# The rolling transfers of the caches, issued inside the forming of a chunk's weights

## The reference, cut to what matters

```
def conv_ffn(h, conv_state, w_up, w_conv, b_conv, w_down):
    u = h @ w_up
    gate, up = u[..., :D_FF], u[..., D_FF:]
    ext = concatenate([conv_state, gate], axis=1)
    conv = ext[:, 0:S] * w_conv[0] + b_conv + ...
    act = silu(conv) * up
    return act @ w_down, ext[:, S:]
...
k_all = concatenate([k_buf, ka], axis=1)
new_k = k_all[:, k_all.shape[1] - keep:]
```

## Time and profile before

| what | value |
|---|---|
| median of three runs | 3106.83 us |
| the profiled execution: its time, and the span of its trace | 3108.89 us, 3107.3 us |
| PE busy | 2867.4 us, 92% of the span |
| DVE, ACT, POOL busy | 1874.3, 1042.3, 675.9 us |
| matmuls of the chunks (L1116), of w_down (L1192) | 673.3 + 252.1 us, 517.8 us |
| POOL idle ahead of L877, the first instruction of form, until weights land | 367.4 us, 32 times |
| rolls: issues, size, median from issue to landing | 8 + 8, 4088 KB, 15.1 and 14.9 us |
| mean granted clock of TensorE, share of full speed | 0.965 |

### The profile page before, as it was taken

How to read it: one execution, slowest core, us unless ns; L and a number is a source line. 1 busy time by engine, 2 the same in 40 slices (tenths; PEclk the granted TensorE clock), 3 DMA queues, 4 the chain that set the end, 5 groups by cost and what they waited for, 6 DMA issues and landing times. The chain is left out here.

```text
span 3107.3 us, 52590 instructions
## 1 busy us (share of the span) xinstructions
PE 2867.4 (92%) x20746; PEld 2630.0 (85%) x20746; DVE 1874.3 (60%) x3293; ACT 1042.3 (34%) x1833; POOL 675.9 (22%) x472
## 2 busy tenths in 40 slices
PE   8999999899898898999989999888998898899998
PEld 7888899689898898999987666555998898899998
DVE  3445344545977777755643444585378778786565
ACT  4444212333322222355533333222242222224544
POOL 3111222003432323101121000141144333330000
PEclk9999999999999999999999999998999999999999
DMA  6211111851244353577712000275213344435776
GB/s 192 60 58 56 36 42 49 324 182 55 80 146 163 122 170 119 176 215 224 216 60 82 15 1 9 99 305 224 68 42 116 129 162 149 135 123 181 221 223 210
DMA packets 280689, 406.87 MB, mean 131 GB/s; under 512 B 21914, under 2 KB 218548, under 8 KB 272884
## 3 DMA queue, kind: packets, MB, share of 16 engines
q1 hardware_dynamic: 272056, 295.32, 29.9%
q0 software_dynamic: 8448, 108.93, 9.8%
HBM read 357.66 MB, written 112.19 MB: 151 GB/s over the span
## 5 line engine op out<-in xcount | busy, mean ns | idle before, releaser
L1116 PE MATMUL psum<-mlp_halves,mlp_operands 128*128 128x352 f32 x3840 | 673.3, 334 | 99.7 <-DVE mlp_combine L1495 89.1
L1116 PEld LDWEIGHTS psum<-mlp_halves,mlp_operands 128*128 128x128 f32 x3840 | 651.8, 198 | 105.5 <-DVE mlp_combine L1495 93.7
L1192 PE MATMUL psum<-mlp_ring 128*128 128x352 f32 x3168 | 517.8, 324 | 6.4 <-issue 3.6
L1192 PEld LDWEIGHTS psum<-mlp_ring 128*128 128x128 f32 x3168 | 511.0, 188 | 8.9 <-issue 6.5
L920 DVE TENSOR_TENSOR mlp_ring<-mlp_ring_whole,mlp_ring 128x864 fp32r<-128x864 f32 x264 | 286.2, 1091 | 205.4 <-ACT mlp_ring L914 204.3
L1905 PE MATMUL psum<-h_ab,w_in_halves 128*128 128x352 f32 x2016 | 341.3, 326 | 3.3 <-PEq L281 2.3
L1905 PEld LDWEIGHTS psum<-h_ab,w_in_halves 128*128 128x128 f32 x2016 | 322.6, 189 | 17.1 <-issue 10.9
L914 ACT CAST mlp_ring<-mlp_ring_whole 128x864 fp32r<-128x864 f32 x264 | 241.1, 915 | 272.8 <-DMA mlp_ring_whole<-products_spill 272.5
L1116 PE MATMUL psum<-mlp_turns,mlp_operands 128*128 128x352 f32 x1440 | 252.1, 324 | 10.1 <-DVE mlp_operands L867 10.1
L1116 PEld LDWEIGHTS psum<-mlp_turns,mlp_operands 128*128 128x128 f32 x1440 | 235.3, 190 | 10.9 <-DVE mlp_operands L867 10.9
L607 PE MATMUL psum<-mlp_halves,project_w 128*128 128x352 f32 x1152 | 189.6, 327 | 8.3 <-DVE project_w L635 8.3
(11 more groups left out here) (372 smaller groups left out, 4311.3 us busy)
## 6 DMA issues: line engine op xcount, KB each, us to landing
mlp_ring_whole<-in_w_down SPq DMA_DIRECT2D x264, 256.0 KB, 2.8
mlp_ring_whole<-products_spill SPq DMA_DIRECT2D x264, 176.0 KB, 3.6
mlp_raw<-in_w_up SPq DMA_DIRECT2D x66, 512.0 KB, 7.0
out_new_a_k_s<-in_cache_a_k POOLq DMA_DIRECT2D x8, 4088.0 KB, 15.1
out_new_a_v_s<-in_cache_a_v POOLq DMA_DIRECT2D x8, 4088.0 KB, 14.9
products_spill<-window SPq DMA_DIRECT2D x44, 528.0 KB, 4.1
w_in_raw<-in_w_in_ab SPq DMA_DIRECT2D x28, 512.0 KB, 4.6
mlp_raw_up<-in_w_up SPq DMA_DIRECT2D x22, 512.0 KB, 3.8
```

Of the source, the lines that this page charges most:

```text
L1116: mm = nc.tensor.matmul(c.bank[bank][:, 0:TILE], operands[:, operand, w, k, :], tokens(x, k), start=begin and k + w + x == 0, stop=end and ...
L1192: mm = nc.tensor.matmul(c.bank[bank_set(at) + o][:, 0:TILE], slot[:, w, o * P:(o + 1) * P], slot[:, x, self.WIDE:], start=k + w + x == 0, ...
```

## The change

The roll is no longer the first thing of the pass. Function form takes a further argument, begun, and calls it after the first of its five instructions; in the pass's first refill, the forming of (g, 1), it issues the roll there, after both waits for the chunk's weights. The wait for the roll moves to the pass's second refill, the forming of (g+1, 0), again ahead of its last sum.

```
-    def form(self, pool, g, s, waits):
+    def form(self, pool, g, s, waits, begun=None):
...
         self.wait_gate(pool, g, s)
         self.wait_up(pool, g, s)
         waits(self.SUM_2)
         tt(into(self.SUM_2), whole(self.UP_1), whole(self.UP_2), ALU.add).then_inc(self.formed, 1)
+        if begun:
+            begun()
         pool.wait_ge(self.formed, done + 1)
...
-                def refill(g, s, next_g, next_s, rolled=None):
+                def refill(g, s, next_g, next_s, begun=None, rolled=None):
...
-                    self.form(pool, next_g, next_s, waits)
+                    self.form(pool, next_g, next_s, waits, begun)
...
                 with pool.Fori(0, DEC_BATCH) as i:
-                    roll.roll(pool, i, call)
-                    refill(i + 2, 0, i + 2, 1, lambda: roll.wait_rolled(pool, i, call))
-                    refill(i + 2, 1, i + 3, 0)
+                    refill(i + 2, 0, i + 2, 1, lambda: roll.roll(pool, i, call))
+                    refill(i + 2, 1, i + 3, 0, None, lambda: roll.wait_rolled(pool, i, call))
```

## The result

The changed kernel takes 2976.97 us in the median of four runs (2973.74 to 2979.97). The kernel before takes 3104.86 us, now over four runs, one more than above (3102.39 to 3109.22): a ratio of 0.9586, interval 0.957 to 0.9603. The prediction was 2978 us, faster.

A forecast was written before the change was run, and what follows sets the result against it. The prediction took the bound to be a gate load waiting out the roll, both released by one event, with PE stalling later. 3106.8 - 129.0 = 2978 us, the added issue and moved wait costed at nothing; range 2968 to 3040 us.

The forecast's parts named there:

- the most to be won: Loops over the groups: sixteen passes take 800.7 us, 671.7 without a stall, so at most 129.0 us to win.
- The gate load's landing: Next gate load, (3, 0), beside the first roll: lands 0.9 to 4.2 us behind the roll's 873.4, taken as 877.
- POOL's spare 0.5 us: POOL asks for the next gate load at 877.5, after P6 of (2, 1), 0.5 us after its forecast landing.
- the 2.3 us to spare: ACT asks for the next gate load at 879.3, for GATE_1, 2.3 us after its forecast landing.
- DVE's room: DVE's seventh sum in an unstalled chunk ends 5.4 us before P2 on PE needs it, a reserve for late loads.
- L + 4.3 - 5.4: PE's wait per pass, gate load L us late for ACT; 4.3 from POOL's sums falling together, 5.4 DVE's room.
- the clock's price: After a PE stall, the next 24 matmuls run at the lower clock, some 1.9 us more per pass.
- The second rival: Part of the stall remains: gate load 3.0 us late for ACT, 3.8 us a pass, 3039 us; chance 0.11.
- The stall that moves unchanged: The roll meets the next gate load, landing at 885.9, 6.6 us late for ACT: 3107 us; chance 0.03.
- the drain one by one: It gets slower: up load, store, gate load follow the roll singly, some 4 us each: 3163 us; chance 0.06.
- The late start of a roll's descriptors: Within the second rival: roll starts 3.4 us later, GpSimd being shut out of its port while writing descriptors.
- the moved wait: Ahead of the last sum of (g+1, 0), some 30 us after the issue, twice the roll's time: costs nothing.

## Why the prediction was right

**What bounds it, and the most to be won.** 129.0 us from the length of a pass against two chunks; the span fell by 128.9. Without the rolls the time is the changed kernel's, so the rolls were all that stood in the pass; with half of their bytes at the old place it is the same again, so it was the late gate load and not the collision as such.

**The gate load's landing.** Predicted 877 in the times before, which run some 0.6 us ahead of those after (835.15 against 835.78): 877.6 in the new ones, measured 877.35. Two terms of it were off and made up for each other. That is luck. The roll took 16.4 to 18.7 us, median 17.2, not 15.0; and the gate load was alone behind it, as the up load had landed at 861.1 and the store some 0.5 us ahead of the roll, so that it landed 1.5 us behind the roll where the forecast had 3.6. With POOL's spare 0.5 us the forecast of no lateness at all was too good: nine of sixteen loads were late for POOL, by up to 1.8 us. For ACT none was late, but of the 2.3 us to spare the worst load left some 0.2.

**DVE's room.** It was the reserve, and the changed kernel never used it: no load was late for ACT, and POOL's lateness ended in POOL's own idle time, which the prediction didn't name. The sum L + 4.3 - 5.4 was worked out from one pass before. Of the experiments that it was not made from, only the roll behind SUM_1 bears it out, for L of 4.4 to 5.7. The roll with the wait left where it was goes against it below that: PE waited 1.27 us at L = 0.05, with DVE behind by its own longer work. A part of the 4.3 us is of this kind too: the two splits took 3.42 us in the pass read, and 1.29 where nothing is late. Of the clock's price, a short wait pays less than 1.9 us: behind 1.28 us the 24 matmuls took 4.08 us, behind 4.39 us 5.67. The second rival, which charged 1.9 us to any wait, was too dear at its low end, and the pass it was read from was milder than the mean of 2.4.

**The rivals.** The stall that moves unchanged and the drain one by one needed the gate load 12.5 us and over 13 us behind the roll; it came 1.5 us behind. Behind the early roll, which lands at 866.9, the up load and the store came 2.0 and 3.3 us later, not one after the other at some 4 us each. The late start of a roll's descriptors did not show: POOL's issue took at most 0.69 us, and the two places among POOL's sums that have no store beside the roll gave rolls of 14.4 to 15.2 and 14.5 to 16.2 us, as the old place did.

**POOL and the moved wait.** The 0.68 us of an issue between two steps of a sum cost nothing that the runs can tell from the version without rolls. The moved wait was costed at nothing and never shows up in the changed kernel's waits in the loops; left where it was, it costs 13 to 18 us, which the prediction didn't price, as the change doesn't leave it there.

## What to carry to other kernels

Look for a large copy and a small load that are released by the same event: here the load landed with the copy, although the two are on different queues. Issue the copy when the load has landed, so that its whole length falls before the next load is due, and move the wait for it behind its landing. Then work out what the next load is late by, engine by engine, and compare it with the idle time of each engine that waits for it and with the room that the last of them has before PE needs its result. Here a load up to 1.8 us late for POOL was free, loads 4.4 us and more late for ACT were not, and a wait of PE of 4.39 us cost 1.7 us more than its length, through the clock. Look also at what a delayed instruction will then run beside: one run lost 13 to 18 us though no load was more than 2.2 us late for ACT.

## What was not expected of the hardware

A roll takes longer with a store issued just ahead of it. The median was 17.2 us with the store 0.34 us ahead in the first pass, 14.7 us with it 3.5 us ahead, and 15.4 us with it 5.1 us behind; in the first of these the store itself took 16.7 us, in the second 4.1. The run with only the issue moved has both cases: its first roll, with the store 0.34 us ahead, took 17.5 us, its second, with the store 7.6 us behind, 15.1. The Trainium skill says that DMAs issued by different engines run on the same DMA engines and interleave (DMA: Bandwidth & Descriptors, "Issuing engines are not separate DMA queues"). The runs agree that the two share: each takes longer beside the other, 17.2 us in place of 14.7 and 16.7 in place of 4.1. Why the store then waits for nearly the whole of the roll was not tried.

The clock does not fall at every stall. The stretches around and behind the wait of 1.28 us, and behind the wait of 4.39 us, follow (the number after POOL's column is the granted clock):

```profile
906.00:909.00 3.00, 1.72 (x12) 1.43 (x10) 3.00 (x4) 1.24 (x2) 1.77 (x1) 1.00 0.98 349
909.00:912.00 3.00, 3.00 (x21) 3.00 (x20) 3.00 (x10) 0.26 (x1) 0.00 (x0) 1.00 1.01 349
```

```profile
908.00:911.00 3.00, 3.00 (x13) 3.00 (x13) 3.00 (x9) 0.00 (x0) 0.00 (x0) 0.58 0.34 92
```

In the first two PE kept its full clock, the level of 2.4 GHz, over the wait and behind it; in the last the mean is 0.58, most of the stretch at the lower level of 1.2 GHz.
